# A new order for the first twenty microseconds of a two-block transformer kernel

## What is computed

```python
def rms_norm(x, g):
    xf = x.astype(jnp.float32)
    y = xf * lax.rsqrt(jnp.mean(xf * xf, axis=-1, keepdims=True) + EPS)
    return (y * g.astype(jnp.float32)).astype(x.dtype)

h = rms_norm(x, g_mix[l])
z = h @ w_in                      # 1024 x 5128
fq, fk, fv, ff, dq, dk, dv, ga, gb = jnp.split(z, splits, axis=-1)
```

## Time and profile before

| | us |
|---|---|
| median of 3 runs | 1813.83 |
| lowest, highest | 1812.6, 1817.23 |
| the profiled execution | 1812.71 |
| its span | 1810.9 |
| TensorE busy in the span | 1756.3 (97%) |
| VectorE busy | 892.5 (49%) |
| ScalarE busy | 618.5 (34%) |
| GpSimd busy | 126.6 (7%) |

### The profile page before, as it was taken

How to read it: one execution, slowest core, us unless ns; L and a number is a source line. 1 busy time by engine, 2 the same in 40 slices (tenths; PEclk the granted TensorE clock), 3 DMA queues, 4 the chain that set the end, 5 groups by cost and what they waited for, 6 DMA issues and landing times.

```text
span 1810.9 us, 25668 instructions
## 1 busy us (share of the span) xinstructions
PE 1756.3 (97%) x10733; PEld 1323.9 (73%) x10733; DVE 892.5 (49%) x1843; ACT 618.5 (34%) x1080; POOL 126.6 (7%) x82
## 2 busy tenths in 40 slices
PE   6999999997999999999999999999999999999998
PEld 5877867886655555555578967667888788888786
DVE  4355554453365555655563577655725532222323
ACT  3334465432111111111252456654624422222222
POOL 1000110221000000000000000011101000000121
PEclk9999999998999999999999999999999999999999
DMA  6511200458999999999926312013421133313201
GB/s 248 203 47 49 92 24 24 140 201 352 409 410 426 426 426 427 426 425 425 398 102 227 113 51 68 1 47 128 163 94 58 48 117 109 109 50 140 93 24 47
DMA packets 76225, 333.55 MB, mean 184 GB/s; under 512 B 6184, under 2 KB 13992, under 8 KB 63177
## 3 DMA queue, kind: packets, MB, share of 16 engines
q1 hardware_dynamic: 72472, 325.04, 45.8%
q0 software_dynamic: 2336, 4.20, 0.6%
q10 hardware_dynamic: 1296, 2.62, 0.4%
HBM read 325.55 MB, written 10.49 MB: 186 GB/s over the span
## 4 chain that ended last, share of the span: by engine, by line
PE 89%; DVE 5%; ACT 3%; issue 1%; DMA 1%; POOL 0%; SPq 0%; DVEq 0%; POOLq 0%; ACTq 0%
PE ps L561 86%; PE ps L980 1%; PE ps L3014 1%; DVE splitr L626 1%; PE ps L2131 1%; DVE arenaf L3096 1%; ACT arenaf L969 0%; DVE arenaf L3114 0%; DMA arenaf<-in_w_out 0%; ACT splitr L637 0%; DVE xf L3405 0%; PE ps L815 0%; DMA xf<-in_x 0%; POOL hr L912 0%; DVE hr L869 0%
## 5 line engine op out<-in xcount | busy, mean ns | idle before, releaser
L561 PE MATMUL ps<-hr,splitr 128*128 128x512 f32 (+1 forms) x2784 | 572.8, 365 | 7.0 <-POOL hr L912 3.8
L561 PEld LDWEIGHTS ps<-hr,splitr 128*128 128x128 f32 x2784 | 471.8, 191 | 87.9 <-issue 6.0
L561 PE MATMUL ps<-splitr,hr 128*128 128x512 f32 (+1 forms) x1488 | 273.9, 343 | 1.0 <-DVE hr L1077 0.8
L561 PEld LDWEIGHTS ps<-splitr,hr 128*128 128x128 f32 x1488 | 234.2, 190 | 34.5 <-DVE hr L1077 1.2
L626 DVE TENSOR_TENSOR splitr<-ring,splitr 128x2048 fp32r<-128x2048 f32 x61 | 142.8, 2342 | 213.0 <-ACT splitr L637 212.9
L2251 DVE TENSOR_TENSOR xf<-xf,ps 128x512 f32<-128x512 f32 x248 | 153.5, 681 | 67.3 <-PE ps L561 67.2
L561 PE MATMUL ps<-arenaf 128*64 128x256 f32 (+7 forms) x1424 | 176.4, 360 | 2.6 <-ACT arenaf L790 1.7
L637 ACT CAST splitr<-ring 128x2048 fp32r<-128x2048 f32 x61 | 116.1, 1906 | 144.4 <-PE ps L561 143.1
L2205 ACT ACTIVATE junkr<-ps,arenaf 64x512 fp32r<-64x512 f32 x62 | 42.3, 682 | 287.8 <-PE ps L561 287.0
L561 PEld LDWEIGHTS ps<-arenaf 128*64 128x64 f32 (+2 forms) x1424 | 107.6, 150 | 43.9 <-issue 12.5
L626 DVE TENSOR_TENSOR splitr<-arenaf,splitr 128x2048 fp32r<-128x2048 f32 x27 | 62.4, 2310 | 101.8 <-ACT splitr L637 101.8
(11 more groups left out here) (421 smaller groups left out, 1960.3 us busy)
## 6 DMA issues: line engine op xcount, KB each, us to landing
arenaf<-in_w SPq DMA_DIRECT2D x23, 2048.0 KB, 15.9
ring<-in_w SPq DMA_DIRECT2D x22, 2048.0 KB, 15.3
splitf<-in_w SPq DMA_DIRECT2D x20, 2048.0 KB, 15.4
hf<-in_w SPq DMA_DIRECT2D x20, 2048.0 KB, 16.4
ring<-in_w_in SPq DMA_DIRECT2D x11, 2048.0 KB, 12.0
otf<-in_w SPq DMA_DIRECT2D x11, 2048.0 KB, 15.4
ring<-in_w_gate_up SPq DMA_DIRECT2D x7, 2048.0 KB, 7.9
arenaf<-in_w_in SPq DMA_DIRECT2D x4, 2048.0 KB, 9.1
```

What stands on the lines that cost most here:

```text
L561: return te.matmul(out, lhsT, rhs, start=start, stop=stop)
```

## The change

The two halves of the first weights are loaded by two transfers, each 256 columns, with a semaphore of its own. SyncE issues tiles 0 and 1, the first half of the weights, tiles 2 and 3, the second half. The constants and parameters are issued by ScalarE, behind its first square root. TensorE turns only tiles 0 and 1 at the start; tiles 2 and 3 are turned behind groups 0 and 1 of the first half of the first projection. TensorE multiplies the identity with itself 8 times before the first turn, 12 times between the two and 38 times after the second; these products go into banks that nobody reads. VectorE and ScalarE take their steps in another order, with the first piece of the weights ahead of tiles 2 and 3.

```diff
--- before.py
+++ after.py
@@ -632,7 +632,7 @@
                     led[1] += 1
                     e, ks, cs, _, _ = pieces[n]
                     hi, lo = piece(n)
-                    for w in se_at(("load", e), *([("piece used", n - 2)] if n > 1 else [])):
+                    for w in se_at(("load", e) if e else ("load", e, n), *([("piece used", n - 2)] if n > 1 else [])):
                         se.wait_ge(*w)
                     se.copy(hi, loaded(e)[:, ks, cs]).then_inc(*se_done("weights high", ("high", n)))
 
@@ -1101,15 +1101,23 @@
 
 
             def sp_start():
-                for t in range(4):
+                def x_in(t):
                     sp.dma_start(X3[:, t, :], io["x"][128 * t:128 * t + 128, :]).then_inc(
                         *sp_done(f"x tile {t}", ("x", t), by=16))
-                    if t == 0:
-                        sp.dma_start(con[:, :], io["con"]).then_inc(*sp_done("constants", ("con",), by=16))
-                        sp.dma_start(par[:, :], io["par"]).then_inc(*sp_done("parameters", ("par",), by=16))
+
+                def first_weights(m):
+                    view, src = entries[0]
+                    ms = slice(256 * m, 256 * m + 256)
+                    sp.dma_start(view(SLOT[place[0]])[:, :, ms], src[:, :, ms]).then_inc(
+                        *sp_done(f"first weights {m}", ("load", 0, m), by=16))
+                x_in(0)
+                x_in(1)
+                first_weights(0)
+                x_in(2)
+                x_in(3)
+                first_weights(1)
                 sp.dma_start(lamv[0:64, :], io["lam"]).then_inc(*sp_done("lambdas", ("lam",), by=16))
                 sp.dma_start(wff, io["w_ff"]).then_inc(*sp_done("forget weights", ("wff",), by=16))
-                sp_load(0)
                 sp.dma_start(oh, io["bucket"]).then_inc(*sp_done("buckets", ("oh",), by=16))
                 sp.dma_start(rl, io["relT"]).then_inc(*sp_done("biases", ("rl",), by=16))
                 for e in (1, 2):
@@ -1122,11 +1130,20 @@
                              vr.rearrange("p (o n) -> p o n", o=1).broadcast_to([128, 8, 1024])).then_inc(
                     *sp_done("bias rows stored", ("vd",), by=16))
 
+            def pe_constants(n):
+                ps = take("constants")
+                holder[where["constants",]] = None
+                for _ in range(n):
+                    mm(ps[:, 0:128], ident, ident, True, True)
+
             def pe_start():
                 for w in pe_at(("con",)):
                     te.wait_ge(*w)
-                for t in range(4):
-                    pe_flip("g_mix", t)
+                pe_constants(8)
+                pe_flip("g_mix", 0)
+                pe_constants(12)
+                pe_flip("g_mix", 1)
+                pe_constants(38)
 
             def ve_start():
                 ve.memset(eps_t, EPS).then_inc(*ve_done("vector step", ("eps",)))
@@ -1136,23 +1153,23 @@
                     ve_tile_recip("g_mix", t)
                     ve_norm("g_mix", X3, 4, H2, "norm", t)
                 scale(0)
+                ve_tile_gains("g_mix", 0)
                 scale(1)
-                ve_tile_gains("g_mix", 0)
+                ve_norm_low("g_mix", H2, 0)
+                ve_tile_gains("g_mix", 1)
+                ve_lead_to(0)
+                ve_norm_low("g_mix", H2, 1)
                 scale(2)
-                ve_tile_gains("g_mix", 1)
-                ve_norm_low("g_mix", H2, 0)
                 scale(3)
-                ve_norm_low("g_mix", H2, 1)
                 ve_tile_gains("g_mix", 2)
-                ve_lead_to(0)
+                ve_lead_to(1)
+                ve_norm_low("g_mix", H2, 2)
                 ve_tile_gains("g_mix", 3)
-                for t in (2, 3):
-                    ve_norm_low("g_mix", H2, t)
+                ve_norm_low("g_mix", H2, 3)
                 for w in ve_at(("rl",)):
                     ve.wait_ge(*w)
                 ve.tensor_copy(thirds(rlx, 8), rl.rearrange("p (h o) -> p h o", o=1)
                                .broadcast_to([33, 8, 16])).then_inc(*ve_done("biases repeated", ("rlx",)))
-                ve_lead_to(1)
                 for w in ve_at(("lam",)):
                     ve.wait_ge(*w)
                 ve.tensor_tensor(lp[0:64, 0:1], lamv[0:64, 0:1], lamv[0:64, 1:2], ALU.mult)
@@ -1163,20 +1180,23 @@
                 for w in se_at(("eps",)):
                     se.wait_ge(*w)
                 sstep(se.activation(norm_small["g_mix"][1][:, 3:4], eps_t, ACT.Sqrt))
+                se.dma_start(con[:, :], io["con"]).then_inc(*se_done("constants", ("con",), by=16))
+                se.dma_start(par[:, :], io["par"]).then_inc(*se_done("parameters", ("par",), by=16))
 
                 def root(t):
                     for w in se_at(("x", t)):
                         se.wait_ge(*w)
                     se_tile_root("g_mix", X3[:, t, :], t, first_squares)
-                for t in range(3):
-                    root(t)
+                root(0)
+                root(1)
                 se_tile_high("g_mix", H2, 0)
+                se_lead_to(0)
+                se_tile_high("g_mix", H2, 1)
+                root(2)
                 root(3)
-                se_tile_high("g_mix", H2, 1)
-                se_lead_to(0)
+                se_lead_to(1)
                 for t in (2, 3):
                     se_tile_high("g_mix", H2, t)
-                se_lead_to(1)
 
             def ge_start():
                 for t in range(4):
@@ -1248,7 +1268,7 @@
 
             def pe_project_diff():
                 tick = ticker(EARLY, pe_early)
-                pe_entry("g_mix", "dq", H2, tick=tick)
+                pe_entry("g_mix", "dq", H2, (0, 1), tick=tick)
                 pe_F("dk", H2, 8, tick=tick)
 
             def ve_project_diff():
```

## The result

Five runs of the changed kernel took 1817.98 to 1824.1 us, median 1821.67; the ratio to the kernel before is 1.0037 with an interval of 1.0024 to 1.005. A second series gave 1821.15, ratio 1.0043 (1.003 to 1.0057). Both intervals lie above 1, so the change costs time. The prediction called a difference under 0.3% none; the first interval takes in that line and the second begins at it. The forecast was 1816 us, +3.1, with a range of 1810 to 1821: its direction was right and its size too small, and the first median lies 0.7 us beyond the upper end. The profiled executions differ by 5.3 us, the medians by 5.9 to 7.8. A few executions at a much lower clock, of 2397 to 3246 us, are left out of all ratios.

A forecast was written before the change was run, and what follows sets the result against it. TensorE was taken to bound the kernel, through its first product's start and the stretch behind it. Start +1.7, clock -1.3, turns +1.8 and bank +0.9 sum to +3.1 us, forecast 1816 us, range 1810 to 1821.

The forecast's parts named there:

- the moment at which the clock rises: TensorE before the first product: the clock rises after the first turn, instructions going from 0.213 to 0.112 us.
- the start: First product on TensorE: starts at 23.4 us against 21.66, +1.7 us, bounds 22.2 to 27.1.
- The bound at 9.9: Latest landing of the constants, in strict order of arrival behind the other traffic; first product then at 27.1 us.
- The third group: Third group of the first products: second weights and tiles 2, 3 in time, 0 us, up to +2.
- turns: Two turns, 16 transposes at 0.112, now stand between the products on TensorE: +1.8 us.
- clock: First 120 products on TensorE run at the high clock from the start, 15.04 instead of 16.30 us: -1.3 us.
- bank: Group "rows" waits for bank 7 until VectorE has copied the first group of dq: +0.9 us (0.7 to 1.1).
- The lower bound of 22.2: Earliest first product on TensorE, with early constants and an early rise of the clock.
- Rival 1: Beginning: constants cover only idle time, first product at 19.3, -1.0 us, 1811.7 to 1812.8; chance 0.22.
- rival 2: Beginning: constants don't raise the clock, first product at 34.4, +17 us, 1830; chance 0.05.
- rival 3: Constants land at 9.9 behind other traffic: first product 27.1, +6.8 us, 1819.5 to 1820.6; chance 0.10 with the fourth rival.
- rivals 4 and 5: Fourth: late second weights stall the third group, +6 by 3 us (0.10 with rival 3). Fifth: unseen gain, below 1808.4 (0.06).

The follow-up runs named there:

- no_constants: The changed kernel without any of the 58 constants; median 1818.15 us, ratio 1.0015 to the kernel before, first product at 19.40 us.
- short_tail: The changed kernel with 22 instead of 38 constants in the last lot; median 1818.44 us, ratio 1.0017 to the kernel before, first product at 22.41 us.
- con_second: The changed kernel with constants and parameters issued by SyncE behind tile 0, not by ScalarE; median 1817.80 us, ratio 1.0016 to the kernel before.
- before_warm: The kernel before with only 4, 2, 3 and 8 constants added behind the turns of tiles 0 to 3; median 1815.78 us, ratio 1.0006.
- early_trim_skip: The changed kernel with constants issued ahead of ScalarE's table load, lots of 4, 3 and 16, and two banks skipped; 1816.47 us, ratio 1.0011 to the kernel before.

## Why the prediction came out as it did

**The mechanism was right.** TensorE's queue of 58 constants and 16 transposes, not the weights, set the first product: no_constants and short_tail moved it as forecast. The price of a constant was right: 38 took 8.65 us (8.5 forecast), from a form that the trace had elsewhere. So, nearly, was the moment at which the clock rises: 8 constants at 0.21 an instruction, 12 at 0.11, the rise itself within the turn between them and not behind it.

**The term that was mis-sized is the start, +1.7 against +3.99**, and in it the landing of the constants. The prediction took "3.9, the same transfer: 6.2 us (5.3 to 9.9)" and they landed at 8.33; from there the row of instructions took 17.3 us (17.2 forecast). The step that was wrong is taking the 3.9 us to landing over from SyncE's queue, with one tile ahead, to a later place behind the first weights: it took 6.0 us. The bound at 9.9 would have given 27.1. The Trainium skill (DMA: Bandwidth & Descriptors, Queues, rings and completion order) says that a DMA engine takes turns between the queues that have work. The prediction's estimate by it was a landing at 7.2 at the most. The measured 8.33 lies between that and the 9.9 of a strict order, and the measurement decides: issued 1.5 us later, with 2 MB issued ahead of it on another queue, the transfer took 1.6 us longer here.

**The smaller terms held**: turns +1.5 for +1.8, clock -1.4 for -1.3, bank +0.78 for +0.9, the last by a wrong reason. The third group did not wait, as forecast. The lower bound of 22.2 for the start comes out at 21.5 by the prediction's own rates (5.3 + 3.0 + 118 x 0.112), and its chances add up to 0.84 for the same and 0.10 for slower, not 0.82 and 0.12; neither touches the forecast.

**What the prediction had no term for** is everything behind 77 us. "Whatever they gain or lose together moves the rest of the kernel as it stands" held in the traces of the changed kernel and of con_second and failed in others: before_warm and early_trim_skip gained 1.8 and 3.7 us in the beginning and nothing in the median. Low stretches of the clock behind 77 us, in other places from kernel to kernel, and the pause at 922 us took the place of the gain in the traces; of the 5.9 to 7.8 us between the medians the beginning explains 4.6 to 4.9, and what the other 1 to 3 us are stays open. Rival 1 (the constants cover only idle time) is out by the 3.5 us between 22.18 and 25.65 and by short_tail; rival 2 (the clock isn't raised) by the first 24 products at 3.11 us; rival 3 (late constants) happened by more than half; rivals 4 and 5 did not.

## What to carry to other kernels

Work put into an engine's queue to fill a wait has to be shorter than the wait in the kernel as it will be, and it delays all behind it when the event that starts it comes late: here the constants' transfer, issued at 2.3 us behind others instead of at 1.2, cost 3.2 of the 4 us (con_second). A group that takes PSUM banks in turn collides when the number of takes between two neighbours becomes the number of banks; count them whenever something is moved in between. A gain of 2 to 4 us in 1800 has to be followed to the end of the trace, place by place, before it is believed or given up.

## What the runs showed of the hardware

- Where the clock falls differs between kernels that have the same products there: granted 0.50 in one trace and 1.00 in another, 1.6 us for each low stretch under full load (24 products in 7.36 instead of 5.78 us). The Trainium skill (TensorE: Matmul & The Clock Gate, Part 1) says that the number of slow products at a kernel's start varies from run to run. What the runs of this case show of that is the mean granted clock of the changed kernel's ten executions, 0.986 to 0.989, with times of 1817.9 to 1824.4 us; its two traces have the low stretches in the same places.
- Idle time of 0.78 us, followed by products of 33 rows, was followed by a fall in four of seven profiled executions; of the seven without that idle time none has a fall there.
- A constant is two instructions, of 0.21 us each at the low clock (the first 16 in the changed kernel) and of 0.11 at the high one; the clock rose during the turn behind the first eight constants, which began at 11.91 us. Transposes, 0.21 us each before it, took 1.04 us for eight behind it.
- Three kernels have a pause of TensorE of 1.8 to 2.2 us at one and the same product and eleven don't. The three have the same number of instructions ahead of it and also come to it first, so which of the two matters is open.
